# Every second transposed block of attention's probabilities leaves PSUM through VectorE instead of ScalarE

## The reference

```python
s = jnp.einsum('btgrd,btkgd->btgrk', q, k_sel).astype(jnp.float32) * HEAD_DIM ** -0.5
dist = (q_pos[None, :, None] - idx).astype(jnp.float32)
s = s - alibi_slopes()[None, None, :, :, None] * dist[:, :, None, None, :]
s = jnp.where(valid[:, :, None, None, :], s, -jnp.inf)
p = jax.nn.softmax(s, axis=-1).astype(v_sel.dtype)
o = jnp.einsum('btgrk,btkgd->btgrd', p, v_sel)
```

## Time and profile before

| what | us |
|---|---|
| median of 3 runs | 1967.34 |
| range of the runs | 1967.07 to 1979.34 |
| the profiled execution | 1974.17 |
| its span, first to last instruction | 1972.4 |
| the prompt's attention in it | about 1262 to 1466 |
| PE busy over the span | 1872.2 |
| DVE busy | 979.0 |
| ACT busy | 598.8 |

### The profile page before, as it was taken

One profiled execution on the slowest core, in us unless ns is written; L12 is line 12 of the kernel. 1 busy time (PEld: TensorE's weight loads), 2 busy tenths in 40 slices (PEclk: granted clock), 3 DMA queues, 4 the chain that ended last, 5 costly groups with the idle time before them and its releaser, 6 DMA issues.

```text
span 1972.4 us, 27613 instructions
## 1 busy us (share of the span) xinstructions
PE 1872.2 (95%) x11014; PEld 1705.3 (86%) x11014; DVE 979.0 (50%) x1579; ACT 598.8 (30%) x912; POOL 235.8 (12%) x236
## 2 busy tenths in 40 slices
PE   5999989999999999999999999899988999999996
PEld 4999988987799999999999999666554499999996
DVE  6401037775786665656465756654552221221365
ACT  6311135653121121111111111366654222122343
POOL 5200000002100000314151610110012000000010
PEclk9999999999999999999999999899999989999998
DMA  6132133311322222323232322423348252212485
GB/s 230 45 90 76 54 86 86 87 48 53 92 84 75 75 64 83 98 87 113 76 120 68 124 76 95 126 63 100 86 134 284 105 186 65 64 56 63 127 241 192
DMA packets 252265, 200.96 MB, mean 102 GB/s; under 512 B 24912, under 2 KB 233416, under 8 KB 249479
## 3 DMA queue, kind: packets, MB, share of 16 engines
q1 hardware_dynamic: 236273, 146.07, 26.2%
q10 hardware_dynamic: 10590, 39.84, 5.3%
q0 software_dynamic: 5312, 13.83, 2.1%
HBM read 156.20 MB, written 43.95 MB: 101 GB/s over the span
## 4 chain that ended last, share of the span: by engine, by line
PE 85%; DVE 5%; ACT 4%; DMA 2%; issue 2%; SPq 1%; ACTq 0%; DVEq 0%
PE ps L353 50%; PE ps L1832 18%; PE ps L1574 4%; PE ps L1705 4%; PE ps L1691 2%; PE ps L1765 2%; PE ps L1794 2%; PE ps L1725 1%; ACT pts L1000 1%; PE ps L1645 1%; PE ps L1815 1%; PE ps L1754 1%; DVE wlo L331 1%; DMA orow<-mix_scratch 1%; DVE score L1251 1%
## 5 line engine op out<-in xcount | busy, mean ns | idle before, releaser
L331 DVE TENSOR_TENSOR wlo<-wraw,whi 128x1024 fp32r<-128x1024 f32 x152 | 196.6, 1295 | 685.9 <-ACT whi L322 685.6
L353 PE MATMUL ps<-ahi,whi 128*128 128x350 f32 (+1 forms) x2112 | 463.7, 325 | 5.9 <-ACT stage L506 3.2
L353 PE MATMUL ps<-alo,whi 128*128 128x350 f32 (+1 forms) x2112 | 460.1, 323 | 0.0
L353 PE MATMUL ps<-ahi,wlo 128*128 128x350 f32 (+1 forms) x2112 | 459.2, 323 | 0.0
L353 PEld LDWEIGHTS ps<-ahi,whi 128*128 128x128 f32 x2112 | 359.9, 190 | 11.5 <-ACT stage L506 4.5
L353 PEld LDWEIGHTS ps<-alo,whi 128*128 128x128 f32 x2112 | 361.2, 189 | 0.0
L353 PEld LDWEIGHTS ps<-ahi,wlo 128*128 128x128 f32 x2112 | 360.8, 189 | 0.0
L1832 PE MATMUL ps<-oparts,whi 128*128 128x384 f32 (+1 forms) x1536 | 325.7, 326 | 5.6 <-DVE oparts L1389 5.6
L322 ACT ACTIVATE whi<-wraw 128x1024 fp32r<-128x1024 f32 x152 | 160.9, 1059 | 493.6 <-PE ps L353 334.1
L1832 PEld LDWEIGHTS ps<-oparts,whi 128*128 128x128 f32 x1536 | 262.8, 189 | 8.0 <-DVE oparts L1389 7.6
L1832 PE MATMUL ps<-oparts,wlo 128*128 128x384 f32 (+1 forms) x768 | 206.0, 322 | 0.0
(11 more groups left out here) (197 smaller groups left out, 1681.2 us busy)
## 6 DMA issues: line engine op xcount, KB each, us to landing
wraw<-w_in SPq DMA_DIRECT2D x88, 512.0 KB, 3.8
wraw<-w_out SPq DMA_DIRECT2D x64, 512.0 KB, 4.0
proj_scratch<-stage ACTq DMA_DIRECT2D x44, 524.0 KB, 2.7
orow<-mix_scratch SPq DMA_DIRECT2D x16, 524.0 KB, 6.8
xt<-x_prompt SPq DMA_DIRECT2D x7, 1024.0 KB, 5.6
qraw<-proj_scratch SPq DMA_DIRECT2D x24, 256.0 KB, 4.4
fh<-x_prompt SPq DMA_DIRECT2D x5, 1024.0 KB, 9.6
y_prompt<-fh ACTq DMA_DIRECT2D x5, 1024.0 KB, 4.6
```

What stands on the lines that cost most here:

```text
L331: nc.vector.tensor_tensor(lo[:, s, :, 0:width], wraw[:, 2 * p + s, :, 0:width], hi[:, s, :, 0:width].bitcast(F32), ALU.subtract).then_inc( ...
L353: last = nc.tensor.matmul(ps[0:width, 3 * pair(n) + c, 0:tn], w[:, s, k, 0:width], m[:, a, t0:t0 + tn], start=(a == 0 and w is hi and m is ...
```

## The change

Blocks with an even number are still copied by ACT, those with an odd number by DVE. The banks and halves of `pts` were already split by parity, so each engine now has its own bank (5 for ACT, 6 for DVE) and its own half of `pts`. The semaphore is split too.

```diff
+        def turned_in(k, parity):
+            t = sum(len(back_blocks(x)) for x in range(k))
+            return [(t + x, v, j) for x, (v, j) in enumerate(back_blocks(k)) if (t + x) % 2 == parity]
...
-                for v, j in back_blocks(k):
-                    i = AUNITS[v][0]
+                for t, v, j in turned_in(k, 0):
                     act.wait_ge(S["p_turned"], t + 1)
-                    if t >= 2:
+                    if t:
                         act.wait_ge(S["pv_mm"], t - 1)
...
+                    nc.scalar.activation(pts[0:kn, 0, 0:w], ps[0:kn, 5, 0:w], ACT.Copy).then_inc(S["pt_copied0"], 1)
...
+            def copy_turned(k):
+                for t, v, j in turned_in(k, 1):
+                    dve.wait_ge(S["p_turned"], t + 1)
+                    if t >= 2:
+                        dve.wait_ge(S["pv_mm"], t - 1)
+                    kn = min(128, L - 128 * j)
+                    w = 4 * rows_of(AUNITS[v][0])
+                    nc.vector.tensor_copy(pts[0:kn, 1, 0:w], ps[0:kn, 6, 0:w]).then_inc(S["pt_copied1"], 1)
...
                 nc.vector.tensor_scalar(peak, peak, -slope(4 * g + r), None, ALU.mult).then_inc(S["amax"], 1)
+                copy_turned(k)
                 if k >= 2:
                     normalize(*divmod(k - 2, 4))
...
+            copy_turned(NHEAD)
             normalize(len(AUNITS) - 1, 2)
+            gate(len(AUNITS) - 3)
+            copy_turned(NHEAD + 1)
             normalize(len(AUNITS) - 1, 3)
-            gate(len(AUNITS) - 3)
+            for k in range(NHEAD + 2, NHEAD + 4):
+                copy_turned(k)
             gate(len(AUNITS) - 2)
+            for k in range(NHEAD + 4, NHEAD + LAG):
+                copy_turned(k)
...
-                pe.wait_ge(S["pt_copied"], t + 1)
+                pe.wait_ge(S[f"pt_copied{t % 2}"], t // 2 + 1)
```

More of the change, by code:

```diff
@@ L258, in build @@
                      "fg_in", "hg_made", "f_scale", "f_act", "f_rms", "f_sqrt", "f_done", "y_out0", "y_out1",
-                     "ak_hi", "ak_lo", "knew_kept", "aqk", "aq_hi", "aq_lo", "p_turned", "pt_copied", "amax", "aexp",
+                     "ak_hi", "ak_lo", "knew_kept", "aqk", "aq_hi", "aq_lo", "p_turned", "pt_copied0", "pt_copied1", "amax", "aexp",
                      "abias", "normed0", "normed1", "inverse", "dist_made", "dist_masked", "sk_turned", "sk_copied", "sqk", "smax", "sexp",
@@ L989, in _ @@
                 nc.scalar.activation(kvtok[0:n, i, :], ps[0:n, i % 6, :], ACT.Copy).then_inc(S["kvtok_kept0"], 1)
-            t = 0
             for k in range(NHEAD + LAG):
-                for v, j in back_blocks(k):
-                    i = AUNITS[v][0]
+                for t, v, j in turned_in(k, 0):
                     act.wait_ge(S["p_turned"], t + 1)
-                    if t >= 2:
+                    if t:
                         act.wait_ge(S["pv_mm"], t - 1)
                     kn = min(128, L - 128 * j)
[L999 to L1002, removed]
+                    w = 4 * rows_of(AUNITS[v][0])
+                    nc.scalar.activation(pts[0:kn, 0, 0:w], ps[0:kn, 5, 0:w], ACT.Copy).then_inc(S["pt_copied0"], 1)
                 if k < NHEAD and k % (4 * KVH) == 4 * KVH - 3 and k // (4 * KVH) + 1 < NTILE:
@@ L1722, in _ @@
                     if t >= 2:
-                        pe.wait_ge(S["pt_copied"], t - 1)
+                        pe.wait_ge(S[f"pt_copied{t % 2}"], t // 2)
                     for h in range(4):
@@ L1736, in _ @@
             pe.wait_ge(S["abias"], NHEAD)
-            pe.wait_ge(S["pt_copied"], blocks_to(len(AUNITS)))
+            for p in range(2):
+                pe.wait_ge(S[f"pt_copied{p}"], blocks_to(len(AUNITS)) // 2)
             for m in range(NSAMP * KVH + 1):
```

## The result

The changed kernel takes 1975.44 us (median of 20 runs, 1973.57 to 1983.39), the kernel before 1969.8 beside it (20 runs). The ratio is 1.0030, 95% interval 1.0021 to 1.0039: 5.6 us longer, within 1% of no change.

A forecast was written before the change was run, and what follows sets the result against it. PE was taken as the bound, busy 186.93 of the attention's 204 us. Terms 2.6 + 0.5 + 0.5 + 0.8 - 1.3 + 1.7 + 1.4 gave +6.2, on the median of 1967.34 a forecast of 1973.5 us, range 1965 to 1983.

The forecast's parts named there:

- the waits are latency: PE's waits for copies are mostly one copy's latency, not a queue on ACT; a second engine helps in few steps.
- the relief: ACT, rid of odd blocks, copies sooner: -0.6 us in step 38, -0.5 in step 46, -0.2 in step 54, sum -1.3.
- Step 54's own -0.2: In step 54 block 77 goes to DVE and needn't wait for ACT: -0.2 us.
- Narrow blocks: Units 0 and 1: DVE's copy stands behind its step's scaled maximum, so products start late: +0.5 and +2.6 us.
- Odd wide blocks: Wide blocks PE waits for pay the copies' difference, 0.09 us: +0.5 first of two, +0.8 alone in a step.
- The split: Steps 54 and 62: DVE's query split stands behind its copies and PE's scores wait: +0.75 and +0.95, sum +1.7 us.
- The end: End of the stage: gates ahead of the last inverse and block 89's copy delay `qz`'s filling: +1.4 us.
- What was to cost nothing: In ordinary steps the copy delays DVE's next addition by up to 1.4 us, but scores need it two steps later.
- Nothing moves: Rival: copies PE waits for mostly stay as late as before, relief cancels the rest; about 0, 1967 us, chance 0.12.
- Relief wins: Rival: freed ACT starts all copies at once, half of PE's 14.6 us goes; -7, 1960 us, chance 0.05.
- VectorE as the bound: Rival: each odd wide copy on DVE is added to PE's path; +25, 1992 us, chance 0.06.
- The clock falls: Rival: PE drops to half speed in unit 1's four steps, up to 5 us more; +11, 1978 us, chance 0.15.

The follow-up runs named there:

- e10: The change, but DVE copies only second blocks of two-block steps (18 to 76), 57 and 67, and unit 15's gate follows the last inverse: -0.06 us against the kernel before.
- e5: The change, with DVE's copies of steps 7 to 14 ahead of the addition of their step: +4.0 us against the kernel before (1.0020).
- e2: The change, but odd blocks from 77 on (step 54 to the end) stay on ACT: +2.2 us against the kernel before (1.0013).
- e3: The change, but only odd blocks 19 to 75 are copied by DVE, the others by ACT: -0.15 us against the kernel before (0.9998).
- e11: The change, but the gate of unit 15 stands behind the last inverse, as in the kernel before: +4.8 us against the kernel before (1.0030).
- e1: The change, but the narrow blocks of units 0 and 1 (0 to 17) stay on ACT: +3.4 us against the kernel before (1.0013).
- e4: The change, but all 90 blocks are copied by DVE, none by ACT: +14.5 us against the kernel before (1.0069).
- e6: The change, with DVE splitting the queries ahead of the copies in steps 54 and 62: +8.7 us against the kernel before (1.0048).
- e8: The changed kernel run once more, unedited: +5.1 us against the kernel before (1.0026).
- e9: The kernel of e6 run once more, unedited (query split ahead of the copies in steps 54 and 62): +3.3 us against the kernel before (1.0021).
- e7: The change, but DVE copies only second blocks of two-block steps (18 to 76), and blocks 57 and 67: +0.8 us against the kernel before (1.0002).

## Why the prediction was right

- **The sum and its place.** Forecast +6.2, measured +5.6 in the medians and +5.7 in the stage. The time of 1973.5 came out 1.9 us low because it was added to the median of three runs, 2.5 us below that of 20; the sum itself was 0.6 too high. That the waits are latency, and that half the copies on another engine would save next to nothing, held: the relief came at steps 38 and 46 alone, -1.0 of the -1.1 given, and e10 has it by itself. Step 54's own -0.2 isn't seen apart from the split.
- **Narrow blocks.** +2.9 of 3.1 (0.4 of it up to step 11, where 0.5 was put between two bounds and not worked out from a row). The reason is shown by e5: the copy behind the addition and maximum of its step is late, ahead of them it isn't. The price for 128x64, taken from a gate of that shape (0.22), was right.
- **Odd wide blocks.** +1.4 of 1.3, at 95 ns a copy instead of 92. The 0.18 us that I had estimated from Perfetto Trace Analysis, section Optimizing Scalar/DVE Operations, in the Trainium skill, isn't what the trace shows.
- **The split.** +1.4 of 1.5 net. Waits for it were to grow to about 3 us, and are 2.8.
- **The end.** +1.0 of 1.4: the sum fair, the reason partly wrong. The step that failed is the one where the gate of unit 15 "now precedes the last inverse" and block 88's copy was to be 0.85 later. It was 0.44 later. The gate alone makes it 0.34 later (e2, e3), since it runs in part while DVE would wait for ACT's exponential; block 87's copy, which I hadn't priced at the end, alone makes it 0.33 later (e11). With that copy in the list the gate's place costs only 0.11. For block 89's copy 0.55 was given, 0.60 measured.
- **What was to cost nothing.** In steps such as 41, 49 and 53 DVE's next addition starts 1.1 to 1.3 us late and a step later the delay is gone. PE's scores wait for additions 1.1 us in 2 waits, before and after.
- **The rivals.** Nothing moves: out, by e1 and e5, each worth 3 us at one place. Relief wins: 1.0 us of the 7. VectorE as the bound: out by e4. The clock falls: not in the profile of the change, whose new waits of 0.9 us lie in just these steps, nor in the five others with the same copies there (e2, e6, e8, e9, e11). Nor is the fall of the earlier trace rows tied to the order of work: e10 has the order of before there. Windows of one microsecond of e10 (length, then PE busy; granted clock third from the end):

```profile
1297.00:1298.00 1.00, 0.34 (x2) 0.30 (x2) 0.93 (x5) 0.72 (x3) 0.00 (x0) 1.00 0.13 38
1298.00:1299.00 1.00, 1.00 (x10) 0.86 (x10) 1.00 (x2) 0.68 (x2) 0.00 (x0) 1.00 0.00 0
1299.00:1300.00 1.00, 1.00 (x5) 0.56 (x3) 0.51 (x1) 0.67 (x2) 0.00 (x0) 1.00 0.00 0
1300.00:1301.00 1.00, 1.00 (x9) 0.92 (x9) 0.88 (x1) 0.00 (x0) 0.00 (x0) 1.00 0.00 0
```

A microsecond with PE busy 0.34 us comes here too, and the clock stays at 1.00 through the stage. Whether e4's waits, up to 2.5 us, brought its falls is open.

## What to carry to other kernels

Ahead of moving work to an idle engine, ask what stands before it in that engine's list when its input is ready, and what stands behind it while it waits; here places in a list made 5.3 us (2.9, 1.4 and 1.0), the slower copies 1.4, and the relief gave 1.0 back. A wait for an engine that was idle when the work came is latency, and a second engine didn't shorten it here; only where the releaser was late because of other work (steps 38 and 46) was there something to gain. A gain or loss of some microseconds in 2000 is read from the length of a stage between two fixed instructions, from step to step; the median of 20 runs confirmed 5.6 us here, that of 12 could not show 0.95.

## What was not expected of the hardware

- The same order of work had the clock at 0.50 for over 3 us in one execution (1303 on in the profile of before, 1.34 us lost) and at 1.00 in others (e1, e3, e10). e7 and e10 differ only behind the addition of step 71, and still e7's profile has the clock at 0.50 twice in steps 2 to 16, which take 41.9 us in it and 37.7 in e10. One of its windows:

```profile
1283.00:1284.00 1.00, 1.00 (x4) 0.74 (x3) 0.00 (x0) 1.00 (x1) 0.20 (x1) 0.50 0.52 164
```

  One profile can't tell whether an edit caused such a fall.
- In 19 of the 36 wide copies of each engine, DVE reads bank 6 while ACT reads bank 5, for 0.16 to 0.26 us. They take 692 and 597 ns at the mean, the 17 others 691 and 596, so this short overlap slows neither; a longer one isn't in these runs.
- On narrow tiles the engines hardly differ (222 and 217 ns for 128x64), so a choice between them there is one of queues alone.
